# Second block of a two-block transformer: the first three tiles behind three of its norms multiply modulated x, and the norm is applied to their products

## The reference

```python
def rms_norm_2(x, w):
    y = xf * lax.rsqrt(jnp.mean(xf * xf, axis=-1, keepdims=True) + EPS)
    return (y * w.astype(jnp.float32)).astype(x.dtype)
...
    for l in range(DEPTH):
        h = rms_norm_2(x, norm1_w[l]) * (1.0 + sc1) + sh1
        x = x + g1 * hybrid_mixer(h, w_in[l], w_out[l], ...)
        h = rms_norm_2(x, norm2_w[l]) * (1.0 + sc2) + sh2
        x = x + g2 * conv_ffn(h, w_gate[l], w_val[l], conv_w[l], conv_b[l], w_down[l])
    return rms_norm_2(x, final_norm_w)
```

## Time and profile before

| what | before |
| --- | --- |
| device time, three runs | median 2201.38 us (2198.02 to 2202.99) |
| profiled execution: span from first to last instruction | 2200.8 us |
| mean granted TensorE clock | 0.971 |
| busy: PE, DVE, ACT, POOL | 95%, 61%, 38%, 11% |
| seam into ffn, layer 0 | begins at 1135.97 us |
| seam into in2, layer 1 | begins at 1507.56 us |
| seam into ffn, layer 1 | begins at 1816.66 us |

### The profile page before, as it was taken

How to read it: one execution, slowest core, us unless ns; L and a number is a source line. 1 busy time by engine, 2 the same in 40 slices (tenths; PEclk the granted TensorE clock), 3 DMA queues, 4 the chain that set the end, 5 groups by cost and what they waited for, 6 DMA issues and landing times.

```text
span 2200.8 us, 26314 instructions
## 1 busy us (share of the span) xinstructions
PE 2087.3 (95%) x10492; PEld 1739.4 (79%) x10492; DVE 1353.3 (61%) x1849; ACT 830.1 (38%) x1230; POOL 243.8 (11%) x224
## 2 busy tenths in 40 slices
PE   4999998989999899999999999999999999999998
PEld 2788787877787777888878888887888887888886
DVE  7676667575666776775476635655685466643554
ACT  3356665324667524223323312324323334322321
POOL 0200111211101222000021000003000012000000
PEclk8899999989999998999999999999999999999999
DMA  8312221224222255442235534533634233433332
GB/s 292 110 58 64 62 68 58 77 77 139 77 59 87 84 146 169 133 134 86 64 90 157 147 104 138 159 109 94 175 97 133 67 92 110 134 111 98 97 95 78
DMA packets 312808, 238.28 MB, mean 108 GB/s; under 512 B 7024, under 2 KB 290032, under 8 KB 312048
## 3 DMA queue, kind: packets, MB, share of 16 engines
q1 hardware_dynamic: 293536, 166.87, 25.8%
q0 software_dynamic: 18432, 67.12, 9.8%
q10 hardware_dynamic: 720, 2.62, 0.4%
HBM read 234.49 MB, written 2.10 MB: 108 GB/s over the span
## 4 chain that ended last, share of the span: by engine, by line
PE 84%; DVE 6%; ACT 5%; issue 3%; DMA 2%; SPq 1%; POOL 0%; DVEq 0%; ACTq 0%; POOLq 0%
PE ps L617 64%; PE ps L592 4%; PE ps L2152 2%; PE ps L1169 1%; ACT a_p L1435 1%; PE ps L1150 1%; PE ps L1151 1%; DMA mod_w_out<-in_ada_w_turned 1%; PE ps L1180 1%; PE ps L2133 1%; DMA start_mod_rows<-in_w_mod_turned 1%; PE ps L2230 1%; ACT L1435 1%; PE ps L1091 1%; PE ps L1040 1%
## 5 line engine op out<-in xcount | busy, mean ns | idle before, releaser
L617 PE MATMUL ps<-h_second_hi,w_hi_second 128*128 128x512 f32 x1120 | 447.3, 399 | 0.3 <-DVE act_value L2560 0.3
L617 PE MATMUL ps<-h_second_lo,w_hi_second 128*128 128x512 f32 x1120 | 437.3, 390 | 0.0
L617 PE MATMUL ps<-h_second_hi,w_lo_second 128*128 128x512 f32 x1120 | 277.0, 389 | 0.0
L575 DVE TENSOR_TENSOR w_lo_second<-w_raw_second,w_hi_second 128x1024 fp32r<-128x1024 f32 x148 | 180.8, 1222 | 108.8 <-ACT w_hi_second L555 108.3
L617 PEld LDWEIGHTS ps<-h_second_hi,w_hi_second 128*128 128x128 f32 x1120 | 210.7, 188 | 45.9 <-issue 3.7
L617 PEld LDWEIGHTS ps<-h_second_lo,w_hi_second 128*128 128x128 f32 x1120 | 210.9, 188 | 44.0 <-issue 1.9
L617 PEld LDWEIGHTS ps<-h_second_hi,w_lo_second 128*128 128x128 f32 x1120 | 210.2, 188 | 44.5
L555 ACT ACTIVATE w_hi_second<-w_raw_second 128x1024 fp32r<-128x1024 f32 x168 | 176.3, 1051 | 111.3 <-PE ps L617 93.8
L617 PE MATMUL ps<-h_hi,w_hi_first 128*128 128x512 f32 (+1 forms) x592 | 208.7, 366 | 3.0 <-ACT proj L1300 1.8
L617 PE MATMUL ps<-h_lo,w_hi_first 128*128 128x512 f32 (+1 forms) x592 | 202.5, 355 | 0.0
L617 PE MATMUL ps<-act_hi,w_hi_down 128*128 128x512 f32 x352 | 136.9, 389 | 0.0
(11 more groups left out here) (305 smaller groups left out, 3809.1 us busy)
## 6 DMA issues: line engine op xcount, KB each, us to landing
w_raw_second<-in_w_in SPq DMA_DIRECT2D x64, 512.0 KB, 4.5
w_raw_first<-in_w_in SPq DMA_DIRECT2D x48, 512.0 KB, 3.9
mod_w_mixer<-in_ada_w_turned POOLq DMA_DIRECT2D x47, 512.0 KB, 3.9
w_raw_second<-in_w_gate SPq DMA_DIRECT2D x44, 512.0 KB, 4.0
w_raw_second<-in_w_val SPq DMA_DIRECT2D x44, 512.0 KB, 4.8
w_raw_down<-in_w_down SPq DMA_DIRECT2D x32, 704.0 KB, 4.8
mod_w_ffn<-in_ada_w_turned POOLq DMA_DIRECT2D x32, 512.0 KB, 4.1
mod_w_in<-in_w_mod_turned POOLq DMA_DIRECT2D x27, 512.0 KB, 3.9
```

The lines of the kernel that those rows point to most:

```text
L575: k.nc.vector.tensor_tensor(lo, raw, hi.bitcast(F32), ALU.subtract).then_inc(k.sem.weight_split_v, 1)
L617: last = tensor.matmul(k.ps[:, bank, 0:count], w[:, q * P:(q + 1) * P], rows[q][:, first:first + count], start=(n == 1), stop=(n == 3 * t.k))
```

## The change

For norms 3, 4 and 5 the first three tiles of the next stage multiply x times gain, without inverse root and shift. Its high and low parts are written row by row while the stage before is still running: `early_row_scalar` (ScalarE: a square and a scaled copy per row) and `early_add_vector`, `early_low_vector` (VectorE: the sum of squares, the low part). `early_tensor` runs the three tiles with lags 0, 3, 5; the squares are summed after its fourth step and the inverse root is spread after its fifth. The shift's share of each product is a constant per output feature: `bias_scalar` multiplies the raw weights by the shift (8 activations of 128x128 for each of the three tiles), `bias_vector` sums the 8 blocks (one reduction of 128x1024), and three matmuls of one column sum over partitions. The true h is still computed meanwhile for the tiles from the fourth on (`early_norm_scalar`, `early_norm_vector`). At the end VectorE multiplies the three products in PSUM by the spread inverse root, and ScalarE adds the constant in PSUM (`finish_early`) ahead of each tile's evacuation. GpSimd's share in these norms and in the low parts of the first weight tiles goes to VectorE. `layer_vectors` is called ahead of the stage instead of ahead of its last tile.

```diff
+                add(("in2", l), n, KT, 1, self.weight_tile("w_in_2", l, n), h2, only_x(EARLY_BANKS[i] if l and i < 3 else 7 if i == 2 else i % 2), "a")
...
+                        add(("ffn", l, half), i, KT, 1, self.weight_tile(name, l, half * FFH + i), h2, only_x(EARLY_BANKS[2 * i + j] if half == 0 and 2 * i + j < 3 else j), "v")
...
-            first = {"in": 3, "in2": 4, "ffn": 0 if t.stage[-1] else 4, "down": 0, "out": 2, "out2": 2}.get(name, KT)
+            first = {"in": 3, "in2": 0 if t.stage[-1] else 4, "ffn": 0, "down": 0, "out": 2, "out2": 2}.get(name, KT)
...
+        elif spent:
+            last.then_inc(spent, 1)
...
+EARLY_BANKS = (3, 4, 5)
+EARLY_LAGS = (0, 3, 5)
+EARLY_SUMS, EARLY_SPREAD = 3, 4
+BIAS_ROWS = (5, 6, 7)
...
+def early_tensor(k, call):
+    s, tensor, own = k.sem, k.nc.tensor, k.stage_tiles[early_stage(call)]
+    rows, biases = early(call)
+    def ready(q):
+        tensor.wait_ge(s.early_low, rows + q + 1)
+    for step in range(KT + EARLY_LAGS[-1]):
+        for n, lag in enumerate(EARLY_LAGS):
+            if 0 <= step - lag < KT:
+                multiply_rows(k, own[n], 0, (step - lag,), ready, None, s.early_spent if n == 2 else None)
+        if step == EARLY_SUMS:
+            tensor.wait_ge(s.early_summed, rows + KT)
+            for q in range(4):
+                last = tensor.matmul(k.ps[:, 2, q:q + 1], k.ssq[:, q * P:(q + 1) * P], k.ones[:, 0:1], start=True, stop=True)
+            last.then_inc(s.norm_summed, 1)
+        if step == EARLY_SPREAD:
+            tensor.wait_ge(s.norm_inverted, call + 1)
+            for q in range(4):
+                over = k.roots[:, q:q + 1].broadcast_to([P, P])
+                last = tensor.matmul(spread_roots(k, TX)[:, q * P:(q + 1) * P], over, k.ident, start=True, stop=True)
+            last.then_inc(s.norm_spread, 1)
+    tensor.wait_ge(s.bias_reduced, biases + 3)
+    for n in range(3):
+        last = tensor.matmul(k.ps[:, 2, 4 + n:5 + n], k.bias_sums[:, n, :], k.ones[:, 0:1], start=True, stop=True)
+    last.then_inc(s.bias_summed, 1)
...
+def early_row_scalar(k, call, stage, n):
+    s, scalar, (rows, _), (gain, _) = k.sem, k.nc.scalar, early(call), early_segment(k, call)
+    x = k.xT[:, n, X_]
+    scalar.wait_ge(*k.evacuated[k.stage_tiles[stage][n]])
+    if n >= 2:
+        scalar.wait_ge(s.early_summed, rows + n - 1)
+    scalar.activation(k.early_squares[n % 2][:, :], x, ACT.Square).then_inc(s.early_squared, 1)
+    scalar.activation(k.h2[0][:, n, :], x, ACT.Copy, scale=gain[:, n:n + 1]).then_inc(s.early_high, 1)
...
+def early_add_vector(k, call, n):
+    s, vector, rows = k.sem, k.nc.vector, early(call)[0]
+    vector.wait_ge(s.early_squared, rows + n + 1)
+    if n:
+        vector.wait_ge(s.early_summed, rows + n)
+    vector.tensor_tensor(k.ssq[:, X_], k.ssq[:, X_], k.early_squares[n % 2][:, :], ALU.add).then_inc(s.early_summed, 1)
+def early_low_vector(k, call, n):
+    s, vector, rows, (gain, _) = k.sem, k.nc.vector, early(call)[0], early_segment(k, call)
+    vector.wait_ge(s.early_high, rows + n + 1)
+    vector.scalar_tensor_tensor(k.h2[1][:, n, :], k.xT[:, n, X_], gain[:, n:n + 1], k.h2[0][:, n, :].bitcast(F32), ALU.mult,
+                                ALU.subtract).then_inc(s.early_low, 1)
...
+def bias_scalar(k, call, n):
+    s, scalar, u, (_, shift) = k.sem, k.nc.scalar, k.stage_tiles[early_stage(call)][n], early_segment(k, call)
+    at = early(call)[1] + n
+    scalar.wait_ge(*k.landed[u])
+    if n == 2:
+        scalar.wait_ge(s.bias_reduced, at - 1)
+    for q in range(KT):
+        cut = slice(q * P, (q + 1) * P)
+        last = scalar.activation(k.bias_products[n % 2][:, cut], k.buffers[u][0][:, cut], ACT.Copy, scale=shift[:, q:q + 1])
+    last.then_inc(s.bias_product, 1)
+def bias_vector(k, call, n):
+    s, vector = k.sem, k.nc.vector
+    vector.wait_ge(s.bias_product, early(call)[1] + n + 1)
+    vector.tensor_reduce(k.bias_sums[:, n, :], k.bias_products[n % 2][:, :].rearrange("p (q m) -> p m q", q=KT), AX,
+                         ALU.add).then_inc(s.bias_reduced, 1)
...
+def early_norm_scalar(k, call, stage):
+    s, scalar, (rows, biases), (_, shift) = k.sem, k.nc.scalar, early(call), early_segment(k, call)
+    own = k.stage_tiles[early_stage(call)]
+    round_tile(k, own[1])
+    early_row_scalar(k, call, stage, KT - 1)
+    round_tile(k, own[2])
+    norm_root(k, call, TX)
+    for q in range(KT):
+        if q == 5:
+            round_tile(k, own[3])
+        scalar.wait_ge(s.normed, 8 * call + q + 1)
+        if q == KT - 1:
+            scalar.wait_ge(s.weight_used, own[2] + 1)
+        else:
+            scalar.wait_ge(s.early_spent, (KT - 1) * rows // KT + q + 1)
+        scalar.activation(k.h2[0][:, q, :], k.norm_tmp2[q % 3][:, :], ACT.Identity, bias=shift[:, q:q + 1]).then_inc(
+            s.h_high, 1)
+    scalar.activation(k.ssq[:, X_], spread_roots(k, TX), ACT.Copy).then_inc(s.early_moved, 1)
+    scalar.wait_ge(s.bias_summed, biases // 3 + 1)
+    scalar.activation(k.early_bias, k.ps[:, 2, 4:7], ACT.Copy).then_inc(s.bias_ready, 1)
+def early_norm_vector(k, call):
+    s, vector, (rows, biases), (gain, shift) = k.sem, k.nc.vector, early(call), early_segment(k, call)
+    own = k.stage_tiles[early_stage(call)]
+    split_tile_vector(k, own[1])
+    early_add_vector(k, call, KT - 1)
+    early_low_vector(k, call, KT - 1)
+    split_tile_vector(k, own[2])
+    norm_invert(k, call, TX)
+    vector.wait_ge(s.norm_spread, call + 1)
+    for turn in range(KT + 2):
+        if turn < KT:
+            if turn >= 3:
+                vector.wait_ge(s.h_low_v, EARLIER_LOWS + rows + turn - 2)
+            vector.scalar_tensor_tensor(k.norm_tmp2[turn % 3][:, :], k.xT[:, turn, X_], gain[:, turn:turn + 1],
+                                        spread_roots(k, TX), ALU.mult, ALU.mult).then_inc(s.normed, 1)
+        if turn >= 2:
+            q = turn - 2
+            vector.wait_ge(s.normed, 8 * call + q + 1)
+            vector.wait_ge(s.h_high, 8 * call + q + 1)
+            vector.scalar_tensor_tensor(k.h2[1][:, q, :], k.norm_tmp2[q % 3][:, :], shift[:, q:q + 1],
+                                        k.h2[0][:, q, :].bitcast(F32), ALU.add, ALU.subtract).then_inc(s.h_low_v, 1)
+    split_tile_vector(k, own[3])
+    vector.wait_ge(s.early_moved, biases // 3 + 1)
+    for n in range(3):
+        product = k.ps[:, k.tiles[own[n]].parts[0][0], :]
+        vector.wait_ge(s.weight_used, own[n] + 1)
+        vector.tensor_tensor(product, product, k.ssq[:, X_], ALU.mult).then_inc(s.early_scaled, 1)
+def finish_early(k, call, n):
+    s, scalar, biases = k.sem, k.nc.scalar, early(call)[1]
+    product = k.ps[:, k.tiles[k.stage_tiles[early_stage(call)][n]].parts[0][0], :]
+    scalar.wait_ge(s.bias_ready, biases // 3 + 1)
+    scalar.wait_ge(s.early_scaled, biases + n + 1)
+    settle_scalar(k, scalar.activation(product, product, ACT.Identity, bias=k.early_bias[:, n:n + 1]))
...
+        if call is not None:
+            if i:
+                early_row_scalar(k, call, stage, i - 1)
+            if i in BIAS_ROWS:
+                bias_scalar(k, call, BIAS_ROWS.index(i))
...
-def linear_vector(k, stage, evacuate=None, last=None):
+def linear_vector(k, stage, evacuate=None, last=None, first=0, call=None):
-        if u + 1 < len(k.tiles):
+        if i >= first and u + 1 < len(k.tiles):
             split_tile_vector(k, u + 1)
+        if call is not None:
+            if i:
+                early_add_vector(k, call, i - 1)
+                early_low_vector(k, call, i - 1)
+            if i > BIAS_ROWS[0]:
+                bias_vector(k, call, BIAS_ROWS.index(i) - 1)
+            if i == BIAS_ROWS[2]:
+                bias_vector(k, call, 2)
...
+        if half == 0 and u < own[3]:
+            finish_early(k, 3 + 2 * l, u - own[0])
...
+        if l and i < 3:
+            finish_early(k, 4, i)
...
+        layer_vectors(k, l, 1)
+        linear_vector(k, ("out2", l), second_residual(k, l, G1, False), call=3 + 2 * l)
+        early_norm_vector(k, 3 + 2 * l)
```

## The result

The changed kernel takes 2208.51 us (median of 4 runs, 2207.13 to 2209.84) against 2200.82 (4 runs, 2198.02 to 2202.99): ratio 1.0036, interval 1.0024 to 1.0049. It is slower by 0.36%, clear of the noise; measured a second time the ratio was 1.0033 (1.0019 to 1.0047). The forecast was 2198.5, faster, with a range of 2188 to 2206; the result lies outside it.

What follows compares the result with a forecast made beforehand. TensorE was taken to bound the kernel (84% of the chain). Seam gains of 5.4 and 4.4, less 0.9 at in2 and 6.0 of clock, made 2.9 us faster: 2198.5 us, range 2188 to 2206.

Steps and rivals of the forecast that it cites:

- Rival C: At the three seams own[4] never waits, so the change does what it is built for: 26 us, 2175.5; chance 0.08.
- 5.4 + 4.4 - 0.9 - 6.0 = +2.9: Gains at the two feed-forward seams, loss at the seam into in2, clock loss behind new waits: 2.9 us faster.
- the clock: Lower granted clock behind TensorE's new waits, taken as 1.5 us each, 6.0 in all.
- the forecast's own bound of 6.8: Most that the lower clock behind four new waits was to cost: 4 x 1.7 us.
- the four places: New TensorE waits: 4.6 us at own[4] of each feed-forward seam, 2.9 at own[1] and 7.7 at own[4] of in2.
- what was put at nothing: Making x rows and reductions during the stage before: VectorE 4.7, ScalarE 4.8 of 5.44 us per `out2` tile, so no cost.
- one of the forecast's own signs of being wrong: Prediction wrong if the last tile's evacuation comes more than 1 us late at a seam into `ffn`.
- Rival D: Strided 128x1024 reduction delays the last tile's evacuation at three seams; at 5.0 us, 8.4 us slower, 2210; chance 0.15.
- the table load: Load of 1.28 us ahead of own[4] at feed-forward seams, said to fall beside VectorE's two taps.
- the start at `in2`: Row 0 of own[1] ready 5.7 us from the seam into in2, a wait of 2.9 us.
- The signs: Named observations at the seams: own[4]'s start and idle time, clock below 0.7, own[1]'s start, reduction at 1.1 to 1.5 us.
- Slower by over 0.2%: Whole kernel over 2205.8 us: most of the slow-reduction rival and a little of the main case; chance 0.13.

Runs made afterwards that it cites:

- the last kernel: Changed kernel with rounds and VectorE splits of own[4] and own[5] moved earlier, own[3] in PSUM bank 7, two reductions moved: 2178.04 us, ratio 0.9898.

## Why the prediction was wrong, point by point

**The mechanism was right in its main part.** The norm left TensorE's path; own[4] waited for ScalarE's round behind evacuations that can't begin until all three products are done and scaled, and the clock fell behind the wait. The runs with the round moved and with TensorE kept busy bear out each. Rival C, the change doing what it can, took more than ScalarE's order (also VectorE's splits, a bank and the reductions): it was 26 us on paper, and the last kernel is 23 us shorter in its stretches, 21.7 by medians.

**Four terms of the sum were too small**, and since gain and loss nearly cancel, they decided the sign. The forecast was 5.4 + 4.4 - 0.9 - 6.0 = +2.9; the stretches gave 3.57 + 2.58 - 4.91 - 7.85 = -6.6, which is 9.5 us worse.

First and largest, *the clock*: "I take 1.5 for each, 6.0", from a row at 0.58 and one at 1.00. It was 2.93, 2.80 and 2.12 behind own[4], and 3.2 behind own[1] at `in2`: 11.0 in all, above the forecast's own bound of 6.8. Each of the four places was paid, at 2.1 to 3.2 us. The row that I priced from had lost 1.7. That makes 5.0 us of the error.

Second, *what was put at nothing*: "They fit, by 0.7", in the part on what costs nothing. With the reduction at 1.25 us, taken from contiguous rows, VectorE's work in the stage before would have fitted; at 1.97 it did not, and the last tile's evacuation began 1.4 us late. That is one of the forecast's own signs of being wrong. Own[1] then waited 0.7 us at each feed-forward seam, and the third tile ended at 19.2 and not at 18.2. The run with neighbouring elements gives back these 1.0 us at each: 2.0 of the error. Rival D named this mechanism and put each microsecond of the third reduction at nearly a microsecond at each seam. Two reductions stand ahead of that evacuation, so 0.76 us on each made 1.0 us in `ffn`, and 3.1 at `in2`, where the clock fell on top.

Third, *the table load*: "falls beside VectorE's two taps here". It didn't. The chain from the third tile's end to own[4] took 11.6 us and not 10.7, which is 1.7 for the two seams, and the run with the load drawn forward gave 1.3 back at each. I had the load's place in the order right and not what it waited for.

Fourth, *the start at `in2`*: own[1]'s wait ended at 6.45 and not at 5.7. The chain from the third tile's end to own[4] was right, 13.7 against 13.8. This leaves 0.8 us of the error. The medians' 7.7 is 1 us more than the stretches' 6.6; the two are not the same executions.

**The signs.** Those that came were the clock (0.50 to 0.62, under 0.7), own[1] at `in2` (6.45, in 5 to 7) and its wait at own[4] (7.4, in 7 to 9). Missed were own[4]'s beginning (30.7 and 38.9, where 28 to 30 and 33 to 37 were named), the wait in `ffn` (5.3, not 4 to 5), own[1] in `ffn` (3.6, not 2.7) and the reduction (1.97, not 1.1 to 1.5).

**The chances.** Slower by over 0.2% had 0.13. Three costs had no row of their own (the clock behind a long wait, the strided reduction, a load behind two waits), and all three came out dearer than taken. The range let them cancel; it should have reached to their sum: 8.9 less 4 x 2.9 of clock, 2 x 1.3 of table load and 2 to 3 of the reduction is 8 us slower, about where the result lies.

## To carry to other kernels

When work is moved ahead of a wait, look at what stands behind the wait in each engine's fixed order, and move that too: a round and a split that were harmless while the first product was done early held up TensorE for 5 to 7 us once all three were done late. Price a wait of TensorE of 3.6 us or more at its length and 2.1 to 3.2 us of low clock on top, as the four places of the changed kernel cost, unless it is kept busy or the wait is removed; by these four the extra doesn't grow with the wait (3.2 behind 3.6 us, 2.1 and 2.9 behind 5.3), and it differs between executions (1.6 behind 3.75 us at own[1] of `in2` in the run with TensorE kept busy). Don't read a difference of 2 us between two profiles as an edit's before looking at where the clock fell in each. A cost that is one in three places near break-even deserves a row of its own shape before it goes into a sum.

## What was not expected of the hardware

A reduction of 128x1024 to 128x128 took 1.97 us with its eight elements 512 bytes apart and 1.21 us with neighbours; an activation of 128x128 took 0.51 instead of 0.39 when it wrote 32 bytes apart, though one started every 0.30 us where it was 0.29. With a second wait on an activation that needs a table, the first wait stood ahead of the table load, and the load lost its overlap, 1.3 us. Behind the same wait of 1.2 us the granted clock was 0.73 in one execution and 1.00 in another, 1.4 us apart. The clock also fell late in the `in2` stretch, where TensorE had no wait, in ten of thirteen profiles, at 1.6 us (once 3) each time.
